# Moving the tie passes and masks of two query tiles from the end of the feed-forward phase into the attention phase

## The reference, cut to what matters

```
score = sum_h w[t,h] * relu(q_idx[t,h] . k_idx[s])      # all admissible keys s <= t
_, sel = top_k(score, 256)                               # each query keeps 256 keys; ties go to the lower key
logits = q . k[sel] / 8 + bias[distance]                 # 8 heads, 2 key/value heads
out = softmax(logits) @ v[sel]
```

## Time and profile before

| | |
|---|---|
| Runs shown | 3960.11, 3965.48 and 6310.45 us; median 3965.48 us |
| Profiled execution | 3957.66 us, its span 3955.8 us |
| Busy share of the span | PE 83%, PEld 46%, DVE 54%, ACT 45%, POOL 43% |
| Chain that ended last, by engine | PE 59%, DVE 17%, issue 7%, ACT 5%, DMA 4%, the rest under 4% each |
| L1340 (search) in that chain | 7% of the span |
| Mean granted TensorE clock | 0.905 of full speed |

### The profile page before, as it was taken

How to read it: one execution, slowest core, us unless ns; L and a number is a source line. 1 busy time by engine, 2 the same in 40 slices (tenths; PEclk the granted TensorE clock), 3 DMA queues, 4 the chain that set the end, 5 groups by cost and what they waited for, 6 DMA issues and landing times.

```text
span 3955.8 us, 57198 instructions
## 1 busy us (share of the span) xinstructions
PE 3279.1 (83%) x19950; PEld 1835.4 (46%) x19950; DVE 2144.8 (54%) x3923; ACT 1794.8 (45%) x2668; POOL 1719.9 (43%) x1292
## 2 busy tenths in 40 slices
PE   4972597799989978899989968799879866999865
PEld 1452345244447452344476532344367742444355
DVE  3625763799115638999244658899944421100155
ACT  0332233555445336554464346554355514554355
POOL 2014202578655024676542033676621014776434
PEclk9995699899999999899999999899989867999866
DMA  2211031223321311232210301232210253232366
GB/s 85 88 32 40 4 101 40 64 90 101 88 77 44 99 37 59 75 101 83 77 65 22 94 27 54 70 106 86 79 35 1 84 164 101 90 105 84 101 195 219
DMA packets 112067, 313.08 MB, mean 79 GB/s; under 512 B 14034, under 2 KB 20514, under 8 KB 111746
## 3 DMA queue, kind: packets, MB, share of 16 engines
q1 hardware_dynamic: 111874, 310.63, 25.2%
HBM read 296.35 MB, written 14.24 MB: 79 GB/s over the span
## 4 chain that ended last, share of the span: by engine, by line
PE 59%; DVE 17%; issue 7%; ACT 5%; DMA 4%; POOLq 3%; POOL 2%; DVEq 2%; SPq 1%; ACTq 0%
PE bank L585 15%; PE bank L587 15%; PE bank L586 15%; DVE spare L1340 7%; PE bank L835 5%; PE bank L824 3%; DVE scores L1573 2%; DVE ring L1308 1%; DMA kT<-in_w_gu 1%; ACT ring L998 1%; DVE R L1627 1%; ACT bank L1138 1%; POOL H L1902 1%; PE bank L810 1%; DVE miss L1343 1%
## 5 line engine op out<-in xcount | busy, mean ns | idle before, releaser
L585 PE MATMUL bank<-H,ring 128*128 128x512 f16 (+2 forms) x2560 | 855.6, 351 | 129.4 <-POOL H L1902 78.1
L586 PE MATMUL bank<-H,ring 128*128 128x512 f16 (+2 forms) x2560 | 855.9, 351 | 0.0
L587 PE MATMUL bank<-H,ring 128*128 128x512 f16 (+2 forms) x2560 | 855.3, 351 | 0.0
L1340 DVE TENSOR_SCALAR_CACHE_REDUCE spare<-scores,cand 128x640 uint8<-128x640 f32 (+4 forms) x448 | 662.5, 1479 | 43.5 <-issue 3.6
L1750 POOL TENSOR_TENSOR ring<-raw,ring 128x1024 f16<-128x1024 f32 (+1 forms) x252 | 487.9, 1941 | 289.9 <-ACT raw L1000 284.5
L998 ACT ACTIVATE ring<-raw 128x1024 f16<-128x1024 f32 (+2 forms) x356 | 348.9, 980 | 390.3 <-PE bank L587 143.9
L585 PEld LDWEIGHTS bank<-H,ring 128*128 128x128 f16 (+1 forms) x2560 | 259.8, 102 | 393.7 <-issue 128.6
L587 PEld LDWEIGHTS bank<-H,ring 128*128 128x128 f16 (+1 forms) x2560 | 261.0, 103 | 246.9 <-issue 8.7
L586 PEld LDWEIGHTS bank<-H,ring 128*128 128x128 f16 (+1 forms) x2560 | 260.2, 102 | 243.3 <-issue 7.4
L1627 DVE CUSTOM_DVE_ANT_0 R<-bank,scores 128x512 f32<-128x512 f32 (+3 forms) x256 | 140.8, 592 | 382.7 <-PE bank L812 373.0
L585 PE MATMUL bank<-R,ring 128*128 128x512 f16 (+1 forms) x880 | 299.0, 355 | 36.7 <-POOL R L1923 25.9
(11 more groups left out here) (296 smaller groups left out, 5966.0 us busy)
## 6 DMA issues: line engine op xcount, KB each, us to landing
raw<-in_w_gu SPq DMA_DIRECT2D x132, 512.0 KB, 3.6
raw<-in_w_in SPq DMA_DIRECT2D x104, 512.0 KB, 3.6
kT<-in_w_gu SPq DMA_DIRECT2D x88, 512.0 KB, 3.8
raw<-in_w_d SPq DMA_DIRECT2D x48, 384.0 KB, 3.2
X<-in_xT SPq DMA_DIRECT2D x8, 2048.0 KB, 9.0
raw<-in_w_d SPq DMA_DIRECT2D x48, 320.0 KB, 3.3
raw<-in_w_out SPq DMA_DIRECT2D x24, 512.0 KB, 3.5
kT<-in_w_d SPq DMA_DIRECT2D x32, 384.0 KB, 3.3
```

Of the source, the lines that this page charges most:

```text
L585: mm(o, lhs[0], rhs[0], start=first, stop=False)
L586: mm(o, lhs[0], rhs[1], start=False, stop=False)
L587: return mm(o, lhs[1], rhs[0], start=False, stop=last)
L1340: v.tensor_scalar(flags[:, 0:128 * (i + 1)], row_of(i), cut_at[:, i % 4:i % 4 + 1], None, ALU.is_ge, ALU.add, accum_out=tally[:, i % 4:i % ...
```

## The change

In the last block the tie work of tiles 14 and 15 leaves `end_search` at the end of F2 and is done by DVE inside A3. `LATE_TIES` names the tile and the unit at which it begins: tile 14 does its count at n = 1 and its four chunks at n = 2 to 5 (units of tile 12); tile 15 does its count at n = 8 and its chunks at n = 9 to 12 (units of tile 13). The instructions are those of before, split into two functions. POOL waits for a new semaphore before its first near mask of tile 14 and of tile 15. The search steps, tiles 12 and 13, and the other blocks stay as they were.

```diff
+LATE_TIES = {14: 1, 15: 8}
-            def end_search(tiles):
+            def count_above(tiles):
                 cols = slice(tiles[0] % 4, tiles[-1] % 4 + 1)
                 for i in tiles:
...
                 v.tensor_scalar(tally[:, cols], tally[:, cols], -1.0, TOPK + 0.5, ALU.mult, ALU.add)
                 dve.drain()
+
+            def keep_best(i, k0, kn):
+                cut, room = (t[:, i % 4:i % 4 + 1] for t in (cut_at, tally))
+                x = row_of(i)[:, k0:k0 + kn]
+                v.tensor_scalar(tie[:, 0:kn], x, cut, None, ALU.is_equal)
+                dve.drain()
+                v.tensor_tensor_scan(rank[:, 0:kn], tie[:, 0:kn], tie[:, 0:kn],
+                                     seen[:, 0:1] if k0 else 0.0, ALU.add, ALU.max)
+                v.tensor_scalar(x, x, cut, OUTSIDE, ALU.is_lt, ALU.mult)
+                dve.drain()
+                v.scalar_tensor_tensor(tie[:, 0:kn], rank[:, 0:kn], room, tie[:, 0:kn], ALU.is_gt, ALU.mult)
+                v.tensor_copy(seen[:, 0:1], rank[:, kn - 1:kn])
+                dve.drain()
+                v.scalar_tensor_tensor(x, tie[:, 0:kn], OUTSIDE, x, ALU.mult, ALU.add)
+                dve.drain()
+
+            def end_search(tiles):
+                count_above(tiles)
                 for i in tiles:
...
+                        keep_best(i, k0, kn)
...
-                    end_search(tiles_of(b))
+                    end_search([i for i in tiles_of(b) if i not in LATE_TIES])
...
+                        for i, first in LATE_TIES.items():
+                            if i // 4 == b and n == first:
+                                count_above([i])
+                            chunk = n - first - 1
+                            if i // 4 == b and 0 <= chunk < len(score_chunks(i)):
+                                keep_best(i, *score_chunks(i)[chunk])
+                                if chunk == len(score_chunks(i)) - 1:
+                                    dve.drain().then_inc(S("late_ties"), 1)
...
+                        if i in LATE_TIES:
+                            pool.wait_ge(S("late_ties"), list(LATE_TIES).index(i) + 1)
```

More of the change, by code:

```diff
@@ L1358, in end_search @@
                 dve.drain()
+            def keep_best(i, k0, kn):
[14 more added lines that the diff above has]
+                count_above(tiles)
                 for i in tiles:
-                    cut, room = (t[:, i % 4:i % 4 + 1] for t in (cut_at, tally))
                     for k0, kn in score_chunks(i):
[L1362 to L1373, removed]
+                        keep_best(i, k0, kn)
             def early_steps(b):
```

## The result

| | kernel before | changed kernel |
|---|---|---|
| Median, beside one another | 3962.19 us (5 runs) | 3937.62 us (5 runs, 3935.38 to 3947.53) |
| Median, a second time (run e0 below) | 3960.62 us (17 runs) | 3946.93 us (12 runs) |
| Profiled execution, span | 3957.66, 3955.8 us | 3936.86, 3934.8 us |
| Chain that ended last | PE 59%, DVE 17% | PE 68%, DVE 8% |

The ratio is 0.9944, 95% interval 0.9928 to 0.996: a gain of 15.8 to 28.5 us. The second time it is 0.9969, 0.9951 to 0.9987: 5.1 to 19.4 us. What both allow is 15.8 to 19.4 us. (One run of before, 6310.45 us, is a disturbed one; it stands in the median of five and in neither ratio.) The change is less than 2%, as predicted, and yet it can be told from no change.

What follows compares the result with a forecast made beforehand. DVE's tie passes of tiles 14 and 15 were taken to hold up A3 alone for about 30 us. 27.6 us gained less 12.0 put in gives 15.6 net: 3944 us on the lowest run, range 3933 to 3960.

Steps and rivals of the forecast that it cites:

- The hand-over: From F2's last eviction to A3's first table load: 6.98 us as one block earlier, table load at 2857.2, gaining 27.6 us.
- n = 4: Third chunk of tile 14 in A3, beside POOL's work on block 2's output: 6.49 us against 2.97 idle, costing 3.52 us.
- n = 5: Last chunk of tile 14 in A3, beside POOL's work on block 2's output: 2.95 us idle, costing 3.54 us.
- n = 10 to 12: Last three chunks of tile 15 in A3: 3.96 us each in 3.47 us of idle time, costing 1.5 us together.
- PE's slow units: Units of A3 after PE waits, where the granted clock can fall: some 1.5 us each, left at nothing in the sum.
- quiet price: DVE's chunk with POOL quiet: 3.96 us for 512 keys, 3.65 us for 384; everywhere, 6.6 us put in.
- worst price: DVE's slowest full chunk with POOL busy, 8.61 us: at n = 4 and 5 gain 11.4 us, everywhere a 7.1 us loss.
- Rival 1: All moved work in A3 hidden because ACT is late in the first units: gain 21 to 25 us, chance 0.14.
- Rival 2: Chunks meet POOL at the worst price, also at n = 9 to 12: gain 0 to 10 us, chance 0.16.
- Rival 4: PE's clock stays down, units 2 to 12 of A3 at 1.2 GHz: slower, up to 4006 us, chance 0.03.
- Rival 5: Hand-over doesn't move: tiles 12 and 13 take 35 us more or something else holds A3; 3958 to 3966, chance 0.03.
- Rival 3: Each lengthened PE wait (n = 4, 5, 8) is followed by a slow unit: 3 x 1.5 us more, 3948 to 3949, chance 0.12.

Runs made afterwards that it cites:

- e0: The changed kernel, unaltered, timed again beside the kernel before and a version with the pieces spread over other units: median 3946.93 us, ratio to before 0.9969.
- e5: Against the changed kernel, POOL's y_newton and y_scale in A3 work on one column instead of 512: 3941.84 us, A3 148.27 us.
- e3: Against the changed kernel, tile 14's count moved to n = 0, its chunks to n = 1, 2, 3 and 7: 3948.01 us, A3 149.77 us.

## Why the prediction was right, step by step

**The hand-over: right to 0.03 us.** 27.57 measured, 27.6 predicted. Tiles 12 and 13 ended at 2845.02, with F2's end 1.67 us later than before: 2843.35 on the clock of before, 2843.3 predicted. That agreement to 0.05 us is luck: their passes began 5.66 us earlier and not 4.75, since the small step behind the counts took 0.17 us in place of 1.07, and took 52.87 us in place of 51.81. Nothing hangs on it, for DVE then had 8.51 us to wait. The step and the first pass, on the DVE timeline of the changed kernel:

```profile
2791.90 0.17 DVE L1358 TENSOR_SCALAR tally<-tally 128x2 f32<-128x2 f32 x1
2792.15 0.49 DVE L1365 TENSOR_SCALAR spare<-scores,cand 128x512 f16<-128x512 f32 x1
```

The hand-over of the block before was the right row, since nothing but the late DVE had differed between the two, and all seven traces with the change give 6.97 or 6.98 us. The range given for the hand-over's place in absolute time was too narrow for the executions: the last eviction alone lies between 2850.2 and 2858.6 in eight traces.

**What is put in: 10.76 us for 12.0, by terms that were off to both sides.**

| Piece | predicted | measured |
|---|---|---|
| n = 1, 2, 9 | 0 | 0, 0.09, 0 |
| n = 3 | 0.7 | 0.74 |
| n = 4 | 3.52 | 3.57 |
| n = 5 | 3.54 | 0.64 |
| n = 8 | 2.65 | 2.79 |
| n = 10 to 12 | 1.5 | 2.61 |
| PE's slow units | 0 | 0.32 net (0.57 of it behind the late mask of n = 8) |
| sum | 12.0 | 10.76 |

That the sum is within 1.2 us is in part luck: n = 5 was priced 2.9 us too high, n = 10 to 12 and the slow units together 1.4 us too low.

*n = 5 is the term that failed.* Its chunk was priced at 6.49 us (it took 5.63) and set against the idle time before the mask alone. But the unit of before held a second wait, which one row of the DVE timeline of before shows:

```profile
2920.97 0.43 DVE L1627 CUSTOM_DVE_ANT_0 R<-bank,R 128x256 f32<-128x256 f32 x1 [1.81 <-POOL R L1868]
```

There DVE waited 1.81 us for POOL's near mask. In the changed kernel the mask of this unit begins so late, because of the chunk at n = 4, that POOL is there first, and the wait is gone. From the start of the mask to the start of the scaling DVE took 2917.38 to 2921.80 = 4.42 us before and 2895.88 to 2898.41 = 2.53 us after, 1.89 less; from there to the next mask 3.23 before and 6.14 after, 2.91 more. The difference is the 1.02 us measured, and the unit behind gives 0.38 of it back: its weight step on DVE took 1.23 us in place of 1.60, because it now comes after POOL's work on the output of block 2 and no longer beside it (1.23 us in e5 too, where POOL is quiet). My sum had counted the delay of n = 4 and n = 5 as if neither could eat a wait of the other. That the wait is eaten by the delay itself shows in e3 too: no chunk at n = 4 or 5, a delay of 1.5 us from the pieces before, and a step of -0.74.

*n = 10 to 12 was priced too low.* The chunk at n = 11 took 4.17 us instead of 3.96, and behind it DVE needs 0.21 us to its own next instruction even when the logits are there, of which I had counted 0.08 (3.96 us is from the start of one chunk to the start of the next): 4.17 + 0.21 - 3.47 = 0.91 us for each, 0.83 to 0.93 measured. So units 11 to 13 came 7.27 and 7.24 us apart, not 6.9. The longer chunk is its first compare, 0.74 us in place of 0.49, beside POOL's near mask (last section). The quiet price was otherwise the right one here, and the worst price was nowhere near.

*The chunk at n = 4 was right for the reason given*: the price taken from the busy stretch, 6.49 us, against 6.70 measured and 3.87 with POOL quiet (e5).

*One sum of the prediction is wrong.* With the worst price at n = 4, 5 and 9 to 12 the terms are 0.7 + 11.3 + 2.65 + 18.5 = 33.2 us, a loss of 5.6 us; the 7.1 us stated count the 1.5 us of n = 10 to 12 twice. The forecast doesn't use it.

**The rivals.** Rival 1, all hidden: no, 10.4 us of the 10.76 is DVE's lateness passed on. Rival 2, mostly given back: no; the pieces at n = 9 to 12 were near the quiet price. Rival 4, the clock stays down: no; the mean granted clock is 0.92 in A3 (2859 to 3013), against 0.94 before (2884 to 3027). Rival 5: no; F2's passes of tiles 12 and 13 took 1.06 us more than before, well within DVE's wait. Rival 3, slow units behind lengthened waits, is half there. Two windows of the changed kernel show the granted clock below the 0.9 that I had named as a sign against me (length, then busy time of PE, PEld, DVE, ACT and POOL, then the clock):

```profile
2896.00:2905.00 9.00, 7.54 (x47) 6.66 (x47) 8.30 (x18) 3.62 (x6) 9.00 (x8) 0.81 0.00 1
...
2914.00:2921.00 7.00, 6.93 (x45) 6.55 (x46) 2.10 (x11) 3.54 (x6) 1.02 (x2) 0.76 0.23 77
```

The first lies behind PE's wait at n = 4. It costs nothing, for DVE was the late one in that unit (the "issue" above). The second lies behind the wait for the mask of unit 8, where PE was the late one, and shows in the chain of the changed kernel:

```profile
2914.59 1.71 PE bank L825 x8
2916.30 3.59 PE bank L836 x26
```

The next unit has 0.87 and 2.90 us, as had this one before: 1.53 of the 1.65 us step. Against it stands a unit that was slow in before, on its chain:

```profile
2987.11 1.04 PE bank L824 x8
2988.15 4.58 PE bank L835 x28
```

After the change its place has 0.87 and 3.13 us, 1.62 us less. So "nothing" for the clock was wrong in its parts and right in its sum, by luck as far as I can see: what moves these slow units is not settled. The length of the wait alone doesn't tell, as three rows of PE's timeline show. PE's wait for the mask of unit 8 in the changed kernel:

```profile
2914.07 0.31 PE L811 MATMUL bank<-kT,q 128*128 128x256 f16 x1 [2.76 <-DVE mx L1636]
```

The same wait in e5, behind which the clock stayed at 1.00:

```profile
2913.25 0.28 PE L811 MATMUL bank<-kT,q 128*128 128x256 f16 x1 [2.76 <-DVE mx L1636]
```

And in before, also followed by 1.00:

```profile
2934.93 0.28 PE L810 MATMUL bank<-kT,q 128*128 128x256 f16 x1 [3.13 <-DVE mx L1627]
```

What PE did earlier differs in the first two: in the changed kernel it had stood 3.75 us at 2896.63 and 1.14 us at 2905.31, in e5 0.92 and 0.51 us. But that doesn't settle it either. In e3 PE stood no longer than 0.91 us in the 29 us before this wait,

```profile
2916.51 0.28 PE L811 MATMUL bank<-kT,q 128*128 128x256 f16 x1 [3.15 <-DVE mx L1636]
```

and yet the granted clock behind it was 0.72 (2916.5 to 2922.5). No run here tells which wait is followed by a slow unit.

**POOL's new semaphore** never held it: its near masks of tiles 14 and 15 are released by `nmax` of DVE or by nothing, none by the tie passes.

**The total.** Stage by stage the change is worth 16.8 us for 15.6 predicted. The median of 3937.62 us lies inside 3933 to 3960 and 6.4 us below 3944: 1.2 us of that is the sum, the rest is the executions' own spread, as the second median, 3946.93 us on the other side, shows.

## What to carry to other kernels

Work moved from a serial end into idle gaps is priced gap by gap: its length beside what will run beside it there, plus the step to the next instruction, less the gap, and less any later wait of the same unit that the delay itself consumes. The gaps should be chosen by that sum, not by order: the same pieces in wider gaps away from POOL cost 2.4 us in place of 10.8. And an effect of ten microseconds in four thousand is measured by the stretches of two traces, cut at events on both sides of the change, sooner than by medians.

## What was not expected of the hardware

- Inside A3, where the mean DMA share is 0.07 (2859 to 3013), the same kernel repeats every unit to 0.02 us in two executions. The stretches outside A3 don't: eight traces put the last eviction of F2 between 2850.24 and 2858.61 and the rest between 839.19 and 848.63 us, in kernels that do nearly the same there. That the weights streamed by DMA make the difference is likely and not shown.
- DVE and POOL slow one another unevenly. At n = 4 the scan took 2.10 for 1.28 us, the step that makes the mask (L1369) 1.43 for 0.46, the last step 1.52 for 0.69. The first compare took 0.48 us there, but POOL's work began only when it was over, at 2889.49. The mask's first instruction, which reads a bank of PSUM and the scores, took 0.69 us while POOL worked beside it. The compare-and-count of 1920 keys took 2.20 us in A3 with a near mask beside it, and 2.21 in F2 with POOL idle. For the first compare and the near mask, the one that began first kept its time: at n = 11 the near mask began at 2951.63 and took 0.73 us, and the compare behind it 0.74; at n = 5 the compare began first, at 2898.61, and took 0.41 us, and the near mask 0.93. On the changed kernel's POOL timeline: the begin of its work at n = 4, a near mask and a pair of y operations beside the chunk of n = 5, a quiet near mask and a pair after them, and the near mask of n = 11:

```profile
2889.49 1.04 POOL L1755 TENSOR_TENSOR mixG<-mixG 128x512 f32<-128x512 f32 x1 [13.92 <-ACT mixG L973]
...
2898.67 0.93 POOL L1888 TENSOR_TENSOR R<-scores,near_bias 128x256 f32<-128x256 f32 x1
2899.56 3.27 POOL L1790 TENSOR_TENSOR H<-H,mixG 128x512 f32<-128x512 f32 x2
...
2907.01 0.73 POOL L1888 TENSOR_TENSOR R<-scores,near_bias 128x256 f32<-128x256 f32 x1 [0.40 <-DVE nmax L1639]
2907.70 2.52 POOL L1790 TENSOR_TENSOR H<-H,mixG 128x512 f32<-128x512 f32 x2
...
2951.63 0.73 POOL L1888 TENSOR_TENSOR R<-scores,near_bias 128x256 f32<-128x256 f32 x1 [4.30 <-DVE nmax L1639]
```

- PE's eight transposes of a unit took 0.87 us, 1.71 us or something between, and which units are slow changed with work that PE itself doesn't do.
